# Two VectorE steps of the mixers given to GpSimd, and the last score tile summed by TensorE

## What is computed

```python
def hgrn2_chunkwise(q, k, v, log_f):
    ...
        bc = jnp.cumsum(gb, axis=2)
        inter = jnp.einsum('bhtc,bhce->bhte', qb * jnp.exp(bc), Sst)
        dec = jnp.exp(jnp.where(causal, bc[:, :, :, None, :] - bc[:, :, None, :, :], -jnp.inf))
        att = jnp.einsum('bhtc,bhsc,bhtsc->bhts', qb, kb, dec)
        o = inter + jnp.einsum('bhts,bhse->bhte', att, vb)

def mlstm_chunkwise(q, k, v, log_i, log_f):
    ...
        s = jnp.einsum('bhtd,bhsd->bhts', qb, kb) * w
        num = a[..., None] * jnp.einsum('bhtd,bhde->bhte', qb, C) + jnp.einsum('bhts,bhse->bhte', s, vb)
        den = a * jnp.einsum('bhtd,bhd->bht', qb, n) + jnp.sum(s, axis=-1)
        h = num / jnp.maximum(jnp.abs(den), jnp.exp(-m_t))[..., None]
    ...

def head_rmsnorm(h, g, n_heads):
    ...
    hf = hf * lax.rsqrt(jnp.mean(hf * hf, axis=-1, keepdims=True) + EPS)
```

## Time and profile before

| | us |
|---|---|
| median of 3 runs | 2472.92 (2472.69 to 2475.2) |
| the profiled execution, device time | 2475.44 |
| its span | 2473.7 |
| TensorE busy in it | 2420.6 (98%) |
| VectorE busy | 1494.5 (60%) |
| ScalarE busy | 1051.7 (43%) |
| GpSimd busy | 121.7 (5%) |

### The profile page before, as it was taken

One profiled execution on the slowest core, in us unless ns is written; L12 is line 12 of the kernel. 1 busy time (PEld: TensorE's weight loads), 2 busy tenths in 40 slices (PEclk: granted clock), 3 DMA queues, 4 the chain that ended last, 5 costly groups with the idle time before them and its releaser, 6 DMA issues.

```text
span 2473.7 us, 29257 instructions
## 1 busy us (share of the span) xinstructions
PE 2420.6 (98%) x11378; PEld 1958.7 (79%) x11378; DVE 1494.5 (60%) x2485; ACT 1051.7 (43%) x1703; POOL 121.7 (5%) x192
## 2 busy tenths in 40 slices
PE   6999999999999999999999999999999999999999
PEld 4878888877878888887887788888788767888886
DVE  5886535777667333346664866633867768555337
ACT  4343334545556333233444423233656654333333
POOL 0000211001010000000000000000011100000000
PEclk9999999999999999999999999999999999999999
DMA  9555566444233233222322233224243313323231
GB/s 371 179 189 192 195 210 120 84 83 115 73 113 121 90 103 102 93 95 88 108 71 75 85 103 102 87 92 136 90 134 106 115 35 102 103 86 102 94 128 68
DMA packets 240219, 286.89 MB, mean 116 GB/s; under 512 B 9641, under 2 KB 223273, under 8 KB 239825
## 3 DMA queue, kind: packets, MB, share of 16 engines
q1 hardware_dynamic: 222752, 230.21, 30.3%
q0 software_dynamic: 15552, 51.62, 6.6%
q10 hardware_dynamic: 1776, 3.18, 0.3%
HBM read 267.12 MB, written 18.09 MB: 115 GB/s over the span
## 4 chain that ended last, share of the span: by engine, by line
PE 81%; DVE 11%; ACT 4%; issue 2%; DMA 1%; POOL 0%; DVEq 0%; ACTq 0%
PE G L2338 68%; PE X L2338 2%; DVE acc L1531 2%; DVE wl L1542 2%; PE G L2836 1%; DVE yl L1580 1%; DVE h L1655 1%; PE G L2366 1%; PE G L2370 1%; PE G L2367 1%; ACT yh L958 1%; PE G L2776 1%; PE X L2817 1%; PE X L2572 1%; PE X L2743 1%
## 5 line engine op out<-in xcount | busy, mean ns | idle before, releaser
L1542 DVE TENSOR_TENSOR wl<-raw,wh 128x1024 fp32r<-128x1024 f32 (+1 forms) x394 | 471.7, 1202 | 633.5 <-ACT wh L887 633.2
L887 ACT ACTIVATE wh<-raw 128x1024 fp32r<-128x1024 f32 (+1 forms) x394 | 406.0, 1037 | 725.2 <-PE G L2338 701.4
L2338 PE MATMUL G<-yh,wh 128*128 128x512 f32 x1696 | 676.3, 399 | 6.8 <-DVE yl L1560 2.1
L2338 PE MATMUL G<-yl,wh 128*128 128x512 f32 x1696 | 661.0, 390 | 0.0
L2338 PE MATMUL G<-yh,wl 128*128 128x512 f32 x1696 | 660.8, 390 | 0.0
L2338 PEld LDWEIGHTS G<-yh,wh 128*128 128x128 f32 x1696 | 318.6, 188 | 78.8 <-issue 10.7
L2338 PEld LDWEIGHTS G<-yl,wh 128*128 128x128 f32 x1696 | 318.4, 188 | 67.4
L2338 PEld LDWEIGHTS G<-yh,wl 128*128 128x128 f32 x1696 | 318.8, 188 | 65.7 <-issue 2.2
L2338 PE MATMUL G<-hidh,wh 128*128 128x512 f32 x704 | 274.0, 389 | 0.0
L2338 PE MATMUL G<-hidl,wh 128*128 128x512 f32 x704 | 273.9, 389 | 0.0
L2338 PE MATMUL G<-hidh,wl 128*128 128x512 f32 x704 | 273.9, 389 | 0.0
(11 more groups left out here) (427 smaller groups left out, 3257.6 us busy)
## 6 DMA issues: line engine op xcount, KB each, us to landing
raw<-in_ffn_w_in SPq DMA_DIRECT2D x44, 1024.0 KB, 4.9
raw<-in_ffn_w_gate SPq DMA_DIRECT2D x22, 1024.0 KB, 5.7
raw<-in_ffn_w_up SPq DMA_DIRECT2D x22, 1024.0 KB, 5.2
ada_c<-in_ada_w POOLq DMA_DIRECT2D x20, 1024.0 KB, 5.7
raw<-in_ffn_w_down SPq DMA_DIRECT2D x16, 1024.0 KB, 4.9
raw<-in_w_in SPq DMA_DIRECT2D x16, 1024.0 KB, 9.9
raw<-in_ffn_w_out SPq DMA_DIRECT2D x16, 1024.0 KB, 4.9
ada_z<-in_ada_w SPq DMA_DIRECT2D x14, 1024.0 KB, 10.8
```

The lines of the kernel that those rows point to most:

```text
L887: nc.scalar.activation(place(wh), src, ACT.Copy).then_inc(hi, 1)
L1542: nc.vector.tensor_tensor(place(wl), src, f32(place(wh)), ALU.subtract).then_inc(lo, 1)
L2338: ins = nc.tensor.matmul(bank, a, b, start=first and i == 0, stop=last and i == 2)
```

## The change

- The clear of `attD` moves from VectorE (L1982) to GpSimd (`zero_levels`). Those for H0 and H1 stand ahead of GpSimd's loop over score tiles, those for H2 and H3 behind M1's last tile. VectorE waits for `att_zero` before its first masked copy.
- The addition of `R` to `acc` moves from VectorE (L2005) to GpSimd (`add_den`): for M0 and M2 behind the affine select of the next head's tile 1, for M1 and M3 behind their own last tile; M1's stands ahead of the clears for H2 and H3.
- `add_rows` adds rows 0 to 2 only; row 3's tile, which has only 128 columns, is summed by one more matmul into the same PSUM columns.
- Semaphores `na_s` and `da_s`, counted one after the other, become one, `scored`.

```diff
+            def zero_levels(x):
+                z = HEADS.index(("H", x))
+                if z:
+                    pool.wait_ge(nd_mm, z)
+                if z == 4:
+                    pool.wait_ge(den_mm, 2)
+                nc.gpsimd.memset(attD, 0.0).then_inc(att_zero, 1)
+
+            def add_den(x):
+                pool.wait_ge(hsq, HEADS.index(("M", x)) + 1)
+                pool.wait_ge(dsq_ready, x + 1)
+                nc.gpsimd.tensor_tensor(acc[:, :], acc[:, :], R[:, :], ALU.add).then_inc(den_added, 1)
...
+                    zero_levels(0)
+                    zero_levels(1)
                     for n in range(NH * TT):
...
-                        for i in ((), (), (1,), (2, 3))[j]:
+                        for i in ((), (), (1,), (2,))[j]:
                             add_rows(x, i)
+                        if x % 2 and j == 1:
+                            add_den(x - 1)
+                        if x % 2 and j == 3:
+                            add_den(x)
+                            if x == 1:
+                                zero_levels(2)
+                                zero_levels(3)
                         if n == 2 * TT - 1:
                             pool.wait_ge(rows_out, 16)
...
                         if i == 1:
-                            if z:
-                                dve.wait_ge(nd_mm, z)
-                            st.do(nc.vector.memset(attD, 0.0))
+                            dve.wait_ge(att_zero, x + 1)
...
-                        if fkind == "M" and f == 1:
-                            dve.wait_ge(hsq, fz + 1)
-                            dve.wait_ge(dsq_ready, fx + 1)
-                            nc.vector.tensor_tensor(acc[:, :], acc[:, :], R[:, :], ALU.add).then_inc(den_added, 1)
...
-                    pe.wait_ge(att_summed, (TT - 1) * (x + 1))
-                    nc.tensor.matmul(G[3][:, P:S], ones[:, :], att_sum[:, P:S], start=True, stop=True)\
+                    pe.wait_ge(att_summed, (TT - 2) * (x + 1))
+                    nc.tensor.matmul(G[3][:, P:S], ones[:, :], att_sum[:, P:S], start=True, stop=False)
+                    nc.tensor.matmul(G[3][:, 3 * P:S], ones[:, :], att[:, 3, 3 * P:S], start=False, stop=True)\
                         .then_inc(den_mm, 1)
```

More of the change, by code:

```diff
@@ L259, in build @@
         att_summed = sem("att_summed")
+        att_zero = sem("att_zero")
         den_mm = sem("den_mm")
@@ L302, in build @@
         av_in = sem("av_in")
-        na_s = sem("na_s")
+        scored = sem("scored")
         na_m = sem("na_m")
@@ L311, in build @@
         qk_lo = sem("qk_lo")
-        da_s = sem("da_s")
         da_m = sem("da_m")
@@ L767, in add_rows @@
                 else:
-                    pool.wait_ge(att_summed, (TT - 1) * x + i - 1)
+                    pool.wait_ge(att_summed, (TT - 2) * x + i - 1)
                 nc.gpsimd.tensor_tensor(att_sum[:, c], att[:, 0, c] if i == 1 else att_sum[:, c], att[:, i, c], ALU.add)\
                     .then_inc(att_summed, 1)
+            def zero_levels(x):
[9 more added lines that the diff above has]
+                nc.gpsimd.tensor_tensor(acc[:, :], acc[:, :], R[:, :], ALU.add).then_inc(den_added, 1)
             def load_halves():
@@ L1292, in qk_upper @@
                 if x >= 12:
-                    act.wait_ge(da_s, 8 * (2 * (x // 6) - 2))
+                    act.wait_ge(scored, 64 + 8 * (2 * (x // 6) - 2))
                 tile, one, two = qk_place(x)
@@ L2000, in mix @@
                         finish(*of)
-                    for fz, fkind, fx, f in FIN.get(s, ()):
-                        if fkind == "M" and f == 1:
-                            dve.wait_ge(hsq, fz + 1)
-                            dve.wait_ge(dsq_ready, fx + 1)
-                            nc.vector.tensor_tensor(acc[:, :], acc[:, :], R[:, :], ALU.add).then_inc(den_added, 1)
                     rows(s)
@@ L2113, in na_add @@
                 for m in range(2):
-                    dve.wait_ge(na_s, 4 * s + 3 + m)
+                    dve.wait_ge(scored, 4 * s + 3 + m)
                     for i in range(2):
@@ L2161, in da_add @@
                     at = 384 - P * qt
-                    dve.wait_ge(da_s, n + 1)
+                    dve.wait_ge(scored, 64 + n + 1)
                     nc.vector.tensor_tensor_reduce(out=pb[:, c, :], in0=X[m][:, :], in1=dbias[:, x % 2, at:at + S],
@@ L2743, in na_scores @@
                         nc.tensor.matmul(X[m][:, UC * i:UC * i + w], aq[r, p, qt * P:(qt + 1) * P],
-                                         ak[r, p, k0:k0 + w], start=True, stop=True).then_inc(na_s, 1)
+                                         ak[r, p, k0:k0 + w], start=True, stop=True).then_inc(scored, 1)
             def na_turn(s):
@@ L2817, in da_scores @@
                     nc.tensor.matmul(X[m][:, :], parts[0][:, c], k, start=True, stop=False)
-                    nc.tensor.matmul(X[m][:, :], parts[1][:, c], k, start=False, stop=True).then_inc(da_s, 1)
+                    nc.tensor.matmul(X[m][:, :], parts[1][:, c], k, start=False, stop=True).then_inc(scored, 1)
             def da_turn(t):
```

## The result

The changed kernel takes 2479.05 us (median of 10 runs), the kernel before 2474.17 us in 10 runs beside them: ratio 1.0021, 95% interval 1.0013 to 1.0029, so **4.9 us more time, 3.2 to 7.2**. The forecast was 2475.9, its range ended at 2478.4, and the sign was right. The profiled execution has a span of 2478.2 us; before it was 2473.7, 4.5 less.

The account below looks back on a forecast made before the run. The prediction took TensorE, busy 98% of the span, as the bound, with short waits for VectorE. +2.56 (earlier gains counted) + 0.22 + 0.22 = +3.0 us on 2472.92 gave 2475.9; range 2471.3 to 2478.4, the forecast's own 2474.8 to 2477.9.

Parts of the forecast that it names:

- the sign: Whole kernel: the change was forecast to make it slower, by +3.0 us.
- H0 and H1: Heads H0 and H1: two clears leave VectorE, so pair tiles come 0.34 and 0.62 us earlier, -0.96 us.
- This is all that can be won: Between 476 and 560 us: TensorE's five listed waits for pair tiles, 1.5 us together, cap the gain.
- The extra matmul: M0 to M3: 0.22 us each; M0's hidden by a 1.67 us wait, M1's, M2's and M3's count.
- M1: M1: -0.2 us from the addition moved to GpSimd, -0.44 at its end from the PSUM sum; -0.64 together.
- The wait at H2: H2: masked copy waits for clear, addition and square; +4.16 us for the wait, +2.56 with earlier gains counted.
- The sum: Whole kernel: +2.56 + 0.22 + 0.22 = +3.0 us, median 2475.9.
- After it: Behind H2's wait: only M2's and M3's extra matmuls cost, +0.22 us each; H3, M3's freed VectorE and DMA nothing.
- The base: Whole kernel: starting median taken as 2472.92 us, with the profiled execution of 2475.44 lying 2.5 above it.
- Rival A: H2: M1's square is done before the copy is due, so no wait; -1.16 us, or 2471.8; chance 0.12.
- Rival B: M1 and M3: GpSimd's additions hold VectorE, up to 2.6 us more; +5.6 us, or 2478.5; chance 0.15.
- The moved DMA: Table's DMA, from 593 to behind H2's values: lands in 27.8 us, cost within a microsecond either way, taken as nothing.

Follow-up runs that it names:

- e3: Kernel before with only the clears moved to GpSimd, additions and sums as before, semaphores merged: 2472.66 us, ratio 0.9998.
- e4: Changed kernel with 24 more matmuls of 512 columns, results unread, where TensorE waits in H2: 2475.27 us, ratio 1.0009.
- e1: Changed kernel with H2's clear put ahead of M1's addition in GpSimd's queue: 2473.04 us, ratio 0.9997.
- e5: e1 with H2's clear made to wait for the square that M1's addition waits for: 2479.91 us, ratio 1.0026.

## Why the prediction went wrong, point by point

- **H0 and H1: right.** Forecast -0.96, measured -1.00 in the changed kernel (-0.3 in H0, -0.7 in H1) and -0.99 in e3, where the clears stand alone. But the listed waits of the matmuls fell by 0.5 us only; the other half came out of spacing between matmuls that is not listed as idle. The weight loads' own waits for pair tiles show more of it: 4.0 us before and 2.7 in the changed kernel, from 476 to 560. "This is all that can be won" was wrong as a rule: the listed waits are no ceiling.
- **The extra matmul: right.** M0's is hidden, M2's and M3's show as +0.22 each.
- **M1: right within 0.2.** Forecast -0.64, measured -0.81. GpSimd's addition took 1.28 us (forecast 1.29); between 582 and 592 TensorE gained 0.26 (forecast 0.2) and at the end 0.54 (forecast 0.44).
- **The wait at H2: right in place, cause and nearly in size.** The chain square, addition, clear, copy is in the trace word for word. Forecast +4.16, measured +3.85. The square started at 601.35 and not at 601.74, since more had been won ahead of it; from the copy's start to TensorE's it was 3.07 us and not 3.20. By this step TensorE would stand at +2.56; counted from 474.71 it stood at +2.04, since the wait was 0.3 us shorter and the gains ahead of it 0.2 larger.
- **The sum: the step that failed.** "After it" lets the work behind the wait run as before. The same prediction said that TensorE's idle time would be near 6 us, and it read the granted clock of the mixer as full; it never asked whether the clock stays full once TensorE stands for so long. This term, +1.95 us in the changed kernel's trace and gone in e4, was taken as 0, without being named. The kernel before had the evidence: its windows at 1314 and 1990, shown above, are at 0.75 and 0.72 of the clock behind idle times of 2 us. With the term, the forecast would have been +5.0, and +4.9 was measured. That the two are so close is partly luck. The steps as measured (-1.00, -0.81, +3.85, +1.95, +0.44) add up to +4.4; the rest lies among the stretches near 700 (+1.6) and 1992 (-1.4), which the prediction knew nothing of and for whose difference no run shows a cause.
- **The base.** Forecast and range stand on a median of 2472.92 from 3 runs; in 10 runs it is 2474.17, 1.25 more. With 4.9 us more than the old base the time would be 2477.8, inside the range and just inside the forecast's own (2477.9). So of the miss of 3.15 us, 1.25 is the base and 1.9 the sum.
- **Rival A: wrong.** The square is not early; the copy waits 4.76 us for GpSimd.
- **Rival B: nearly the right size (+5.6) for a wrong reason.** In M1 the two did not meet: GpSimd's addition ran beside a conv tap and a score tile, which read PSUM, and took 1.28 us. GpSimd's mask behind it takes 1.22 us beside VectorE's split, but so it did in the kernel before (1.23 at 586.38). In M3 they met, and each held the other a little. M1, then M3:

```profile
582.90 1.28 POOL L785 TENSOR_TENSOR acc<-acc,rstd 128x512 f32<-128x512 f32 x1 [1.86 <-ACT acc L1202]
582.95 0.75 DVE L1801 SCALAR_TENSOR_TENSOR mqk<-G,vec,mqk 128x509 f32<-128x509 f32 x1
...
710.55 0.77 DVE L1978 TENSOR_TENSOR mol<-mo,moh 128x512 fp32r<-128x512 f32 x1
...
710.76 1.71 POOL L785 TENSOR_TENSOR acc<-acc,rstd 128x512 f32<-128x512 f32 x1
...
712.11 0.90 DVE L1978 TENSOR_TENSOR mol<-mo,moh 128x512 fp32r<-128x512 f32 x1
```

  The addition, begun 0.21 us behind a VectorE product, takes 1.71 us instead of 1.26; the product that VectorE begins while the addition still runs takes 0.90 instead of 0.68. No score tile is late by it: TensorE's offset behind M3's sums grows by the 0.22 of the matmul alone. This agrees with the Trainium skill, page "SBUF — State Buffer", section "Who interferes with whom": of a VectorE instruction with two SBUF inputs and a GpSimd instruction that reads SBUF, the first blocks the other.
- **The moved DMA: right in its cost.** It lands after 27.6 us. A weight load issued beside it takes 17.0 us to land, where the kernel before has a median of 4.9 at this place, but no wait for a weight load appears up to 728.

## What to carry to other kernels

Before work is moved to an idle engine, read what its queue holds: a cheap instruction (0.52 us) put behind one that waits for a late input inherits that wait, and here swapping the two gave back all of the 4.9 us (e1). A new wait of the matmul engine is to be priced twice, as its length and as what the clock costs behind it, and a part of what is saved of such a wait may be paid back to the clock (in e5, 0.5 of 1.2 us). Count offsets of the same instruction between two traces from a common point, since medians of runs could not tell parts of 0.1 to 1 us apart.

## What the runs showed of the hardware that was not expected

- **TensorE's clock.** Behind idle times of 4.39, 5.59 or 5.60 (three traces) and 7.93 us the granted clock was at its lower level, 1.2 GHz, for 6.8, 6.8 and 10.2 us, of which part fell into the work behind; the cost was 2.46, 1.95 and 2.65 us. Behind 1.99 to 2.41 us of idle time it fell for 3.4 us in some executions and not in others, at a cost of 1.4 to 1.7 us each. Matmuls whose result nobody reads held it at 2.4 GHz through the whole wait (e4). The Trainium skill, page "TensorE: Matmul & The Clock Gate", Part 1, says that the halved clock is the default and that activity releases it. The traces agree: the clock fell in all five with an idle time of 4.39 us or more, and stayed up in e4, where matmuls filled the same wait.
- **These stretches are a part of the scatter of the times.** Three traces of the unchanged kernel before had two (1315, 1992), two (696, 1315) and none of them, apart from one near 1155 and those of the first 65 us and of the end, which every trace has. The three executions took 2475.44, 2473.24 and 2470.65 us.
